# A hybrid encoder layer on one core: the delta net's two key heads on the two partition halves, and changes at the kernel's head and tail

## What is computed

```python
def step(S, inp):
    q_c, k_c, u_c, w_c, a_c, gc_c = inp
    v_new = u_c - jnp.einsum("bhld,bhde->bhle", w_c, S)
    o = (jnp.einsum("bhld,bhde->bhle", q_c * jnp.exp(gc_c)[..., None], S)
         + jnp.einsum("bhij,bhje->bhie", a_c, v_new))
    g_last = gc_c[..., -1]
    S = (S * jnp.exp(g_last)[..., None, None]
         + jnp.einsum("bhld,bhle->bhde", k_c * jnp.exp(g_last[..., None] - gc_c)[..., None], v_new))
    return S, o
```

## Time and profile before

| | |
|---|---|
| median of 3 runs | 2723.81 us (2723.58 to 2724.0) |
| the profiled execution | 2722.52 us |
| its span, first to last instruction | 2720.8 us |
| mean granted clock of TensorE | 0.998 of full speed |
| PE busy / DVE / ACT / POOL | 99% / 57% / 44% / 1% |
| DMA | 497 MB, 183 GB/s on the mean |

### The profile page before, as it was taken

One profiled execution on the slowest core, in us unless ns is written; L12 is line 12 of the kernel. 1 busy time (PEld: TensorE's weight loads), 2 busy tenths in 40 slices (PEclk: granted clock), 3 DMA queues, 4 the chain that ended last, 5 costly groups with the idle time before them and its releaser, 6 DMA issues.

```text
span 2720.8 us, 36735 instructions
## 1 busy us (share of the span) xinstructions
PE 2688.6 (99%) x14728; PEld 2227.5 (82%) x14728; DVE 1556.1 (57%) x1717; ACT 1210.7 (44%) x1351; POOL 29.9 (1%) x62
## 2 busy tenths in 40 slices
PE   8999999999999999999999999999999999999998
PEld 6888888888888777888888888888888888888886
DVE  5555555545467685848656655665655555555444
ACT  5444444444456355535445443443444444444443
POOL 0000000000000000000000000000000000000000
PEclk9999999999999999999999999999999999999999
DMA  6666666666676454454576565544566666666664
GB/s 211 190 189 188 189 188 190 190 190 192 178 210 184 148 180 139 139 157 140 156 258 229 186 185 186 189 152 139 182 191 187 190 188 190 189 188 206 193 193 142
DMA packets 260195, 497.34 MB, mean 183 GB/s; under 512 B 17881, under 2 KB 28364, under 8 KB 259692
## 3 DMA queue, kind: packets, MB, share of 16 engines
q1 hardware_dynamic: 250528, 470.21, 57.2%
q0 software_dynamic: 4496, 16.40, 1.8%
q10 hardware_dynamic: 5052, 9.03, 0.9%
HBM read 482.99 MB, written 12.60 MB: 182 GB/s over the span
## 4 chain that ended last, share of the span: by engine, by line
PE 93%; DVE 4%; ACT 2%; issue 1%; ACTq 0%; DMA 0%; POOL 0%; DVEq 0%; POOLq 0%
PE pp L321 28%; PE pp L323 28%; PE pp L322 28%; PE pa L374 1%; DVE wlo L282 1%; PE pa L837 1%; PE pa L1833 1%; PE pb L1818 1%; ACT whi L277 0%; PE pa L383 0%; DVE vg L1205 0%; DVE qk L1205 0%; PE pb L1063 0%; PE pa L1058 0%; ACT tmp L1476 0%
## 5 line engine op out<-in xcount | busy, mean ns | idle before, releaser
L282 DVE TENSOR_TENSOR wlo<-raw,whi 128x1024 fp32r<-128x1024 f32 (+1 forms) x888 | 1080.9, 1220 | 931.2 <-ACT whi L277 924.6
L277 ACT ACTIVATE whi<-raw 128x1024 fp32r<-128x1024 f32 (+1 forms) x888 | 935.7, 1056 | 1333.7 <-PE pp L323 1314.0
L321 PE MATMUL pp<-whi,xhi 128*128 128x512 f32 (+1 forms) x2208 | 871.4, 395 | 1.0 <-DVE xlo L405 1.0
L323 PE MATMUL pp<-wlo,xhi 128*128 128x512 f32 (+1 forms) x2208 | 857.7, 388 | 0.0
L322 PE MATMUL pp<-whi,xlo 128*128 128x512 f32 (+1 forms) x2208 | 857.3, 388 | 0.0
L321 PEld LDWEIGHTS pp<-whi,xhi 128*128 128x128 f32 x2208 | 414.7, 188 | 90.9 <-issue 5.4
L323 PEld LDWEIGHTS pp<-wlo,xhi 128*128 128x128 f32 x2208 | 414.6, 188 | 86.5
L322 PEld LDWEIGHTS pp<-whi,xlo 128*128 128x128 f32 x2208 | 415.0, 188 | 81.4
L321 PE MATMUL pp<-whi,hhi 128*128 128x512 f32 x704 | 274.3, 390 | 0.0
L323 PE MATMUL pp<-wlo,hhi 128*128 128x512 f32 x704 | 273.9, 389 | 0.0
L322 PE MATMUL pp<-whi,hlo 128*128 128x512 f32 x704 | 273.9, 389 | 0.0
(11 more groups left out here) (390 smaller groups left out, 2030.3 us busy)
## 6 DMA issues: line engine op xcount, KB each, us to landing
raw<-in_ffn_w_gate SPq DMA_DIRECT2D x176, 512.0 KB, 3.8
raw<-in_ffn_w_up SPq DMA_DIRECT2D x176, 512.0 KB, 3.8
raw<-in_ffn_w_down SPq DMA_DIRECT2D x176, 512.0 KB, 3.7
raw<-in_w_in SPq DMA_DIRECT2D x144, 512.0 KB, 4.1
raw<-in_w_lift SPq DMA_DIRECT2D x32, 512.0 KB, 5.0
raw<-in_w_out SPq DMA_DIRECT2D x32, 512.0 KB, 4.3
raw<-in_w_mk SPq DMA_DIRECT2D x32, 512.0 KB, 4.3
raw<-in_w_mv SPq DMA_DIRECT2D x32, 512.0 KB, 4.4
```

The source lines that it names most:

```text
L277: nc.scalar.activation(whi[:, s, :, 0:width], raw[:, s, :, 0:width], ACT.Copy).then_inc(whi_ready, 1)
L282: nc.vector.tensor_tensor(wlo[:, s, :, 0:width], raw[:, s, :, 0:width], whi[:, s, :, 0:width].bitcast(F32), ALU.subtract).then_inc(wlo_rea ...
L321: nc.tensor.matmul(out, a_hi[:, k0 + k, tok], w_hi, start=first, stop=False)
L323: mm = nc.tensor.matmul(out, a_hi[:, k0 + k, tok], w_lo, start=False, stop=final)
```

## The change

In the delta net the partitions no longer hold two chunks but the two key heads (and with each its two value heads, index `e`), and the four chunks lie along the free axis. Each step of a chunk then uses all 128 partitions, half as many elements per partition on DVE and ACT, and PE's products alternate between `halves` = partitions 0 to 63 and 64 to 127. Two value heads of one key head are taken in one product where the left operand is the same. Keys and values are turned by products with the identity instead of by transposes, since each chunk goes to both halves. The scalars (decay, beta) are laid out the same way. z of the first half is written to DRAM and read back in the new layout. The tables of background steps and slots are changed with it.

At the head the first vector (`ffn1_norm`) is loaded alone by ACT, straight away, and turned alone; all other vectors go over POOL's queue and are turned after the first eight slots. ACT's function table is loaded in advance.

At the tail the last residual and its squares are done in two halves, the root's table is loaded in advance, the weight is multiplied into the first three quarters during the last projection, and the last scaling is divided between DVE (three quarters) and ACT (one, which it also stores).

The core of the diff:

```diff
@@ gdn_pe: turning, matrices
-                for kk in range(2):
-                    nc.tensor.transpose(bank[2][:, tt, kk * P:(kk + 1) * P], qk[:, 2 + kk, tok], ident[:, :])
-                for kk in range(4):
-                    mm = nc.tensor.transpose(bank[tt][:, kk // 2, (kk % 2) * P:(kk % 2 + 1) * P], vg[:, kk, tok], ident[:, :])
+            for c in range(NCH):
+                tok = slice(c * C, (c + 1) * C)
+                for p, r in enumerate(halves):
+                    nc.tensor.matmul(heads4[2][r, c, :], qk[:, 2 + p, tok], ident[:, :], start=True, stop=True)
+                for e in range(2):
+                    for p, r in enumerate(halves):
+                        mm = nc.tensor.matmul(heads4[c // 2][r, 2 * (c % 2) + e, :], vg[:, 2 * p + e, tok], ident[:, :], start=True, stop=True)
...
-            for u in range(8):
-                tt, hl = u // 4, u % 4
-                for cp in range(2):
-                    nc.tensor.matmul(units[2][r, u, :], qk[:, 2 + hl // 2, tok], kb[:, hl, tok], start=True, stop=True)
-                    mm = nc.tensor.matmul(units[3][r, u, :], qk[:, 2 + hl // 2, tok], qk[:, hl // 2, tok], start=True, stop=True)
+            for c in range(NCH):
+                for p, r in enumerate(halves):
+                    nc.tensor.matmul(units[2][r, 2 * c:2 * c + 2, :], qk[:, 2 + p, tok], kb[:, 2 * p:2 * p + 2, tok], start=True, stop=True)
+                for p, r in enumerate(halves):
+                    mm = nc.tensor.matmul(units[3][r, c, :], qk[:, 2 + p, tok], qk[:, p, tok], start=True, stop=True)
@@ gdn_pe: one chunk
-                for hl in range(4):
-                    mm = nc.tensor.matmul(heads4[0][r, hl, :], qk[:, 2 + hl // 2, tok], s_g[:, c % 2, hl, :], start=True, stop=True)
+                for p, r in enumerate(halves):
+                    mm = nc.tensor.matmul(heads4[0][r, 0:2, :], qk[:, 2 + p, tok], s_g[:, c % 2, 2 * p:2 * p + 2, :], start=True, stop=True)
...
-                for hl in range(4):
-                    mm = nc.tensor.matmul(heads4[1][r, hl, :], ut_g[r, 4 * tt + hl, :], r_g[r, hl, :], start=True, stop=True)
+                for e in range(2):
+                    for r in halves:
+                        mm = nc.tensor.matmul(heads4[0][r, 2 + e, :], ut_g[r, 2 * c + e, :], r_g[r, e, :], start=True, stop=True)
...
-                for hl in range(4):
-                    mm = nc.tensor.matmul(heads4[3][:, hl, :], kn[r, tt, (hl // 2) * P:(hl // 2 + 1) * P], vs_g[r, hl, :],
-                                          start=True, stop=True)
+                for p, r in enumerate(halves):
+                    mm = nc.tensor.matmul(heads4[1 + 2 * p][:, 0:2, :], kn[r, c, :], vs_g[r, :, :], start=True, stop=True)
...
+                for e in range(2):
+                    for p, r in enumerate(halves):
+                        nc.tensor.matmul(heads4[2][r, e, :], qe[:, 2 * p + e, tok], s_g[:, c % 2, 2 * p + e, :], start=(e == 0), stop=False)
+                for e in range(2):
+                    for r in halves:
+                        mm = nc.tensor.matmul(heads4[2][r, e, :], att[r, 2 * c + e, :], vn_g[r, e, :], start=False, stop=(e == 1))
@@ scalars_pe
-                nc.tensor.transpose(pb[:, 2, 8 * tt:8 * tt + 8], gc_t[0:GHV, tok], ident[0:GHV, 0:GHV])
-                mm = nc.tensor.transpose(pb[:, 2, 16 + 8 * tt:24 + 8 * tt], beta_t[0:GHV, tok], ident[0:GHV, 0:GHV])
+                for n, src in enumerate((gc_t, beta_t)):
+                    for r in halves:
+                        at_ = GHV * (NCH * n + c)
+                        mm = nc.tensor.matmul(pb[r, 2, at_:at_ + GHV], src[0:GHV, tok], ident[0:GHV, 0:GHV], start=True, stop=True)
@@ POOL
+            g.dma_start(z_dram.rearrange("(t p) c -> p t c", p=P), z_nat[:, :, :]).then_inc(sem("z_loaded"), 16)
+            pool.wait_ge(sem("z_loaded"), 16)
+            fetch_z(z_dram)
             fetch(0, gs, "gs_loaded")
@@ tables (slots of the same projections, moved)
-    "gdn1.naturals": 2, "gdn1.ks0": 1, "gdn1.vnew0": 1, "gdn1.vnew1": 1, "gdn1.vnew2": 1, "gdn1.vnew3": 1,
+    "gdn1.naturals": 1, "gdn1.ks0": 1, "gdn1.state0": 1, "gdn1.state1": 1, "gdn1.state2": 1, "gdn1.state3": 1,
...
-    "inv0.rows": 10, "inv0.10": 2, "inv0.20": 1, "inv0.30": 1, "inv0.40": 1,
+    "inv0.rows": 12, "inv0.10": 1, "inv0.20": 1, "inv0.30": 1, "inv0.40": 1,
...
-    "inv1.rows": 9, "inv1.10": 1, "inv1.20": 1, "inv1.30": 1, "inv1.40": 1,
+    "inv1.rows": 12, "inv1.10": 1, "inv1.20": 1, "inv1.30": 1, "inv1.40": 1,
@@ head
-            g.memset(nat[:, :, :], 0.0).then_inc(prm_clear, 1)
-            pool.wait_ge(prm_clear, 1)
+            for half in range(2):
+                for name, src, m in prm_sources(A):
+                    r = PRM[name]
+                    if r // P == half and r > 0:
+                        g.dma_start(nat[r % P:r % P + m, half, 0:src.shape[-1]], src).then_inc(PRM_LOADED[half], 16)
...
-            act.wait_ge(prm_clear, 1)
+            act.dma_start(gs[0:KT, 0, 0:P], A["ffn1_norm"][0].rearrange("(m p) -> m p", p=P)).then_inc(sem("gain_loaded"), 16)
+            nc.scalar.preload_act_table(ACT.Silu)
...
                 multiply_normed(pe, gu[0], gu[0]["free"], "f1norm", live, 1)
+                prm_turn(pe, 0)
                 prm_turn(pe, 1)
@@ tail
-            last_sumsq(act, prods["f2dn"][3], 5)
+            nc.scalar.preload_act_table(ACT.Sqrt)
+            for tt in range(TT):
+                act.wait_ge(sem(last["released"][0]), last["released"][1] + tt)
+                op = nc.scalar.activation(gs[:, tt, :], h[:, tt, 3 * CW:4 * CW], ACT.Square, accum_out=ss[:, tt, 3:4])
+            op.then_inc(sumsq_ready, 1)
             norm_root(act, 5)
+            act.wait_ge(rstd_ready, 6)
+            act.wait_ge(sem("gained"), 1)
+            for tt in range(TT):
+                op = nc.scalar.activation(h[:, tt, 0:CW], h[:, tt, 0:CW], ACT.Copy, scale=rstd[:, tt:tt + 1])
+            op.then_inc(sem("first_out_ready"), 1)
+            act.wait_ge(sem("first_out_ready"), 1)
+            act.dma_start(out_cols(0), h[:, :, 0:CW]).then_inc(stored, 16)
...
+            nc.vector.tensor_tensor(nat[:, :, :], h[:, :, 3 * CW:4 * CW], fgain[:, 3 * CW:4 * CW].unsqueeze(1).to_broadcast([P, TT, CW]),
+                                    ALU.mult).then_inc(sem("gained"), 1)
             norm_scale(dve, 5)
-                    op = nc.vector.scalar_tensor_tensor(h[:, tt, cols], h[:, tt, cols], rstd[:, tt:tt + 1], fgain[:, cols], ALU.mult, ALU.mult)
+                    op = nc.vector.tensor_scalar(part[:, tt, :], part[:, tt, :], rstd[:, tt:tt + 1], None, ALU.mult)
```

More of the change, by code:

```diff
@@ L638, in ffn_dve, with final_gain @@
                         x_low(dve, then, c - 1)
+                    if c > 0 and j == 12 and then is None:
+                        final_gain(dve, c - 1, h[:, :, (c - 1) * CW:c * CW])
+        def final_gain(dve, c, dst):
+            dve.wait_ge(sem("fgain_loaded"), 16)
+            dve.wait_ge(sumsq_ready, NDC * 5 + c + 1)
+            cols = slice(c * CW, (c + 1) * CW)
+            nc.vector.tensor_tensor(dst, h[:, :, cols], fgain[:, cols].unsqueeze(1).to_broadcast([P, TT, CW]),
+                                    ALU.mult).then_inc(sem("gained"), 1)
         def residual(dve, pr, c, scale):
@@ L757, in build @@
         heads4 = [b.rearrange("p a (u c) -> p (a u) c", c=GH) for b in bank]
+        halves = [slice(e * C, (e + 1) * C) for e in range(2)]
         def over_units(mask):
@@ L982, in scalars_dve @@
         def scalars_dve(dve):
-            dve.wait_ge(sem("scalars_turned"), 1)
-            nc.vector.tensor_copy(scal[:, 0:32], pb[:, 2, 0:32]).then_inc(sem("scalars_ready"), 1)
+            dve.wait_ge(sem("aux_turned"), 2)
+            for n in range(2):
+                for p, r in enumerate(halves):
+                    src = pb[r, 2, 32 * n:32 * n + 32].rearrange("p (c h q) -> p h c q", c=NCH, h=HALVES)[:, :, :, 2 * p:2 * p + 2]
+                    op = nc.vector.tensor_copy(scal[r, 16 * n:16 * n + 16].rearrange("p (h c e) -> p h c e", h=HALVES, c=NCH), src)
+            op.then_inc(sem("scalars_ready"), 1)
         def aux_act(act):
@@ L1075, in gdn_pe @@
             pe.wait_ge(sem("g_out"), n)
-            for kk in range(4):
-                for tt in range(TT):
-                    mm = nc.tensor.transpose(pa[:, kk, tt * P:(tt + 1) * P], nat[:, tt, kk * P:(kk + 1) * P], ident[:, :])
+            for u in range(8):
+                mm = nc.tensor.transpose(heads4[u // 4][:, u % 4, :], nat[:, u // 4, (u % 4) * P:(u % 4 + 1) * P], ident[:, :])
             mm.then_inc(sem("g_out_turned"), 1)
@@ L1218, in gdn_dve @@
             dve.wait_ge(sem("gr_loaded"), 16 * n)
-            for tt in range(TT):
-                for cp in range(2):
-                    r = slice(cp * C, (cp + 1) * C)
-                    tok = slice(tt * P + cp * C, tt * P + (cp + 1) * C)
-                    own = gc_n[r, tt, 4 * hf:4 * hf + 4].unsqueeze(2).to_broadcast([C, 4, C])
```

(44 more changed lines are left out.)

146 lines of the change are left out of this document (80 added, 66 removed), and 41 rows, old and new, of tables (SLOTS_ACT, SLOTS_DVE, STEPS).

## The result

| | before | changed |
|---|---|---|
| median of runs, us | 2723.69 (2723.44 to 2724.0, 4 runs) | 2698.72 (2698.34 to 2698.98, 4 runs) |
| profiled execution, us | 2722.52 | 2698.83 |
| its span, us | 2720.8 | 2697.1 |
| first product starts | 16.51 | 11.50 |
| residual of the last product to the end | 13.2 | 11.45 |

The ratio is 0.9908, 95% interval 0.9891 to 0.9925: 25.0 us faster between the medians and 23.7 between the profiled executions. The forecast was 2699.0. Its parts weren't all right, though: two errors of 5.0 and 3.4 us had opposite signs, and the reason for the 1.3 added for the median was not the one assumed, as far as the traces show. As the interval is 4.6 us wide to either side, I read single microseconds from blocks in the traces and use the medians as a check.

The account below looks back on a forecast made before the run. TensorE, busy 2688.6 of 2720.8 us, was taken as the bound. Delta-net work -20.3, waits +1.7, head -4.9 and +0.2, tail -1.5 sum to -24.8: 2722.5 becomes 2697.7, plus 1.3 gives 2699.0; range 2695 to 2703.

Parts of the forecast that it names:

- the 1.3 added for the median: Whole kernel: the median of runs, 2723.81, lies 1.3 us above the profiled execution, so 1.3 is added at the end.
- The overlap of the halves: Delta net: products on opposite partition halves run at once, 0.054 us per instruction of 128 columns instead of 0.127.
- rival (a): Delta net: pairs contracting over all 128 rows don't overlap; about 2712 us, chance 0.08.
- Rival (e): Delta net: dealing blocks to both halves doesn't save what RWKV rows promise, only head and tail gain; 2718 us, chance 0.03.
- The saving of a chunk: Delta net: TensorE's blocks of a chunk shrink from 5.1 to 2.25 us, saving 2.85, or 22.8 over eight chunks.
- The waits: Delta net: TensorE waits on VectorE add 2.4 and 1.8 us, those before L837 go (-2.5); net +1.7.
- rival (c): Delta net: everything is covered and TensorE's waits vanish; 2695 us, chance 0.08.
- Rival (b): Delta net: VectorE sets the chunk's pace, some 1.2 us at each of eight chunks instead of 0.5; 2705 us, chance 0.18.
- Turning, matrices, scalars: Delta net: turning keys and values into rows +2.7 us, the chunk matrices -1.4, the scalars +1.2.
- Head: Kernel start: first product at 11.6 instead of 16.51, -4.9 us; two small turnings moved later, +0.2.
- Tail: Kernel end: stores end last, so only the earlier first issue counts (-0.5); together -1.5 us, ends -1 and -3.
- Rival (d): Head: POOL's 17 load issues go slowly beside VectorE and turning the parameters stalls TensorE; slower, 2736 us, chance 0.04.

Follow-up runs that it names:

- the doubled blocks: Keys by state and solve issued twice in each chunk, in either kernel: kernel before 2737.39 against 2723.58 us; changed kernel 2706.1 us, +7.5.
- the doubled state: The changed kernel with VectorE's four operations of the new state issued twice: 2705.32 us, +6.7.

## Why the prediction was right, and where it wasn't

- **The overlap of the halves** was right, full height included; rival (a) is out by the rows of L1070 and L1081 and by the doubled blocks. Rival (e) falls with it.
- **The saving of a chunk** was mis-sized: 2.85 forecast; 2.09 measured with the wait for the state, 2.22 without it, so 17.8 over eight chunks instead of 22.8. The step that failed is "about 0.127 us for one instruction of 128 columns". I had divided a block of 1.02 by its eight instructions. The doubled blocks show 0.107 for an instruction and, per block, an edge of 0.16 inside a run of blocks (1.02 - 0.86 before, 0.59 - 0.43 after) or 0.26 between projections. Only the instructions are halved: 5 x 0.43 = 2.15 for a chunk. The 0.1 that I set for all edges of a chunk should have been some 1.0. (The state update doesn't write one half of the partitions, as I had it: it contracts over one half and writes all 128. Its halves overlap as well, by the rows of L1081.)
- **The waits** were mis-sized too, the other way and in good part by the same step. I let the outputs cover 0.87 of the state's chain; with their edges they cover 1.17, and 0.13 is left where I had 0.4 (0.8 us in all instead of 2.4). Before the solve I had 0.3 for each of six; there is none, since a split of 1.22 behind the state and the two operations of 0.42 just fit (VectorE's r_g ends at 916.09, the solve starts at 916.39). With -2.7 for L837 (forecast -2.5) and +0.2 before L813 the waits brought -1.7 instead of costing 1.7. This is rival (c), which I had at 0.08, in all but the 0.8. Blocks and waits together: -21.1 forecast, -19.5 measured. Rival (b), VectorE as the pace, is out by the doubled state.
- **Turning, matrices, scalars**: +3.0, -1.5, +0.7 measured for +2.7, -1.4, +1.2 forecast.
- **RWKV and rest**: I had counted 0 to +1; it was -0.5 and -0.4.
- **Head**: -4.9 + 0.2 forecast, -5.0 in the medians. The first product (11.6 forecast, 11.50 measured) and the issue of x as the bound were right. What I hadn't seen in the timeline of before is the slow pace behind the first product.
- **Tail**: -1.5 forecast; 11.45 and 13.2 in the timelines give -1.75, the medians -1.7. The stores run one behind the other, and only the first issue counts. The reciprocal was done 3.15 after the residual started (3.35 forecast), and the first store was issued 0.94 later (0.95 forecast).
- **Rival (d)**: POOL issues its 17 loads from 2.37 to 10.9, 0.50 each, whether VectorE works beside it or not (POOL's timeline: 0.48 at 3.52 beside an idle VectorE, 0.50 at 7.91 beside a busy one). TensorE doesn't wait for them. The rule of the Trainium skill ("SBUF — State Buffer", section "Who interferes with whom") didn't show in these issues. They are no full test of it either: it speaks of VectorE's two-port modes, and gives the splits (`tensor_tensor`), which ran beside the issues from 9.0 on, no such mode.
- **The median**: adding 1.3 was right as arithmetic and wrong as a reason. As far as the traces show, it stood for slow products that the profiled execution of before had not drawn. Without it the forecast would have been 2697.7, 1.0 below. Between the profiled executions, which drew three and nine, 1.2 of the 24.8 are missing for the same reason.

So the mechanism was right. Two terms were off, mostly by the same error, and by luck nearly cancelled: 5.0 us too much from the blocks, 3.4 too much for the waits. The 1.6 that were left came back in small pieces: -0.3 in the turning, matrices and scalars together, -0.9 in what I had put at nothing, -0.3 in the head and -0.2 in the tail.

## What to carry over

A block's time is so many instructions times their pace, plus an edge that no packing removes; get the two apart before scaling, by two blocks of different length or by issuing one twice. When a block shrinks, compute the cover that it gives to others with its edge too. And look at the distance between the first products of a kernel before comparing two single traces: work that nobody needs can be worth its place while TensorE waits for its first data.

## What the hardware showed

- Two products for opposite column halves of the array run at once although both contract over all 128 rows: doubled keys by state cost 0.054 us for 128 columns, against 0.107 on one half. They need not alternate: TensorE started a product of the other half ahead of three earlier instructions, two products of a half in a row cost nothing (0.68 for the solve in either order), three and four cost 0.3 to 0.5 for a block, twelve cost the overlap (5.41 against 3.20).
- After the start TensorE ran 0.43 us for 512 columns, its level of 1.2 GHz, and then 0.23, the level of 2.4 GHz, while the granted clock stood at 1.00. The view of TensorE by stretches shows both for the changed kernel (stretch, length, busy time and products, granted clock, DMA share, GB/s); seven products touch the 2.5 us to 15.5, twelve the next:

```profile
13.00:15.50 2.50, 2.50 (x7) 1.00 1.07 372
15.50:18.00 2.50, 2.50 (x12) 1.00 1.04 381
```

  The number of slow products was 3 to 10 in kernels with the same head, after a wait of 2.3 to 2.6 us for x; with TensorE at work from 1.6 on it was 0 in both runs. The Trainium skill, "TensorE: Matmul & The Clock Gate", "Part 1: The HAM clock gate (the "warmup" mystery)", says that the chip sets this level by how busy TensorE has been; the two runs in which it was kept busy agree.
- POOL's selections for the masks took 0.23 us each in the kernel before, with VectorE idle, and 0.94 to 1.15 between 14.44 and 17.8 in the changed one, beside VectorE's splits, where nobody waited for them. From 12.94 to 14.1, beside VectorE's scaling of x out of PSUM (L395), they still took 0.23 to 0.25. POOL's issues of loads did not slow (0.50 to 0.53 beside the splits).
